# An RWKV-7 and sliding-window block on one core: the recurrence's first corner moves behind KB's products, and the moments ahead of its copy

## The reference, cut to what matters

```python
def step(S, inp):
    r_t, w_t, k_t, v_t, kk_t, a_t = inp
    sa = jnp.einsum('bhvk,bhk->bhv', S, -kk_t)
    S = (S * w_t[:, :, None, :]
         + sa[..., None] * (kk_t * a_t)[:, :, None, :]
         + v_t[..., None] * k_t[:, :, None, :])
    return S, jnp.einsum('bhvk,bhk->bhv', S, r_t)
...
mean = jnp.mean(o, axis=-1, keepdims=True)
var = jnp.mean(jnp.square(o - mean), axis=-1, keepdims=True)
o = ((o - mean) * lax.rsqrt(var + GN_EPS)).reshape(B, T, W)
```

## Time and profile before

| | us |
|---|---|
| runs, lowest, median, highest of 3 | 1305.36, 1310.01, 1314.89 |
| profiled execution | 1319.53 |
| its span in the trace | 1317.7 |
| TensorE busy (share of the span) | 1269.1 (96%) |
| VectorE busy | 829.4 (63%) |
| ScalarE busy | 480.1 (36%) |
| GpSimd busy | 271.8 (21%) |
| mean granted clock of TensorE | 0.975 of full speed |

### The profile page before, as it was taken

One profiled execution on the slowest core, in us unless ns is written; L12 is line 12 of the kernel. 1 busy time (PEld: TensorE's weight loads), 2 busy tenths in 40 slices (PEclk: granted clock), 3 DMA queues, 4 the chain that ended last, 5 costly groups with the idle time before them and its releaser, 6 DMA issues.

```text
span 1317.7 us, 20551 instructions
## 1 busy us (share of the span) xinstructions
PE 1269.1 (96%) x8207; PEld 1040.8 (79%) x8207; DVE 829.4 (63%) x1247; ACT 480.1 (36%) x863; POOL 271.8 (21%) x210
## 2 busy tenths in 40 slices
PE   7999999989899999999999999999999999999996
PEld 6888888655688888778878888888888887888885
DVE  6856522289766877364485665666777676546765
ACT  6100033398422323233463333333333334333334
POOL 0465600034311112110003332233133200000001
PEclk9999999999987989699999999999999999999998
DMA  5576532300222232152213223214544577766643
GB/s 217 186 250 219 209 116 93 109 1 18 48 57 48 52 72 58 31 204 106 80 49 128 70 74 96 96 55 154 176 154 150 192 241 270 257 206 215 208 144 136
DMA packets 117627, 172.80 MB, mean 131 GB/s; under 512 B 55328, under 2 KB 59424, under 8 KB 117280
## 3 DMA queue, kind: packets, MB, share of 16 engines
q1 hardware_dynamic: 117536, 171.54, 39.4%
HBM read 119.57 MB, written 51.39 MB: 130 GB/s over the span
## 4 chain that ended last, share of the span: by engine, by line
PE 80%; DVE 9%; DMA 5%; ACT 3%; issue 2%; POOL 0%; SPq 0%; DVEq 0%; ACTq 0%; POOLq 0%
PE bank L2366 28%; PE bank L363 21%; PE bank L2470 14%; PE bank L468 2%; PE bank L1491 2%; PE bank L1416 2%; DMA hid_scratch<-rt 1%; PE bank L377 1%; PE bank L1262 1%; DMA inv_scratch<-LM 1%; DMA X<-inv_scratch 1%; PE bank L986 1%; DVE scores L1172 1%; PE bank L1497 1%; DMA v_scratch<-vo 1%
## 5 line engine op out<-in xcount | busy, mean ns | idle before, releaser
L2366 PE MATMUL bank<-thi,ahi 128*128 128x512 f32 x320 | 124.5, 389 | 0.0
L2366 PE MATMUL bank<-tlo,ahi 128*128 128x512 f32 x320 | 124.5, 389 | 0.0
L2366 PE MATMUL bank<-thi,alo 128*128 128x512 f32 x320 | 124.5, 389 | 0.0
L2470 PE MATMUL bank<-ch,dwh 128*128 128x512 f32 x308 | 120.4, 391 | 1.3 <-DVE dwl L2044 1.2
L2470 PE MATMUL bank<-ch,dwl 128*128 128x512 f32 x308 | 119.9, 389 | 0.0
L2470 PE MATMUL bank<-cl,dwh 128*128 128x512 f32 x308 | 119.9, 389 | 0.0
L342 DVE TENSOR_TENSOR ring_wlo<-ring_raw,ring_whi 128x1024 fp32r<-128x1024 f32 x30 | 40.1, 1336 | 124.4 <-ACT ring_whi L336 124.4
L363 PE MATMUL bank<-hhi,ring_whi 128*128 128x512 f32 x288 | 114.8, 399 | 0.0
L363 PE MATMUL bank<-hhi,ring_wlo 128*128 128x512 f32 x288 | 112.4, 390 | 0.0
L363 PE MATMUL bank<-hlo,ring_whi 128*128 128x512 f32 x288 | 112.3, 390 | 0.0
L2366 PE MATMUL bank<-x1hi,ahi 128*128 128x512 f32 x240 | 93.4, 389 | 0.0
(11 more groups left out here) (341 smaller groups left out, 2826.7 us busy)
## 6 DMA issues: line engine op xcount, KB each, us to landing
hraw<-hid_scratch SPq DMA_DIRECT2D x12, 1024.0 KB, 6.5
hid_scratch<-hid SPq DMA_DIRECT2D x22, 512.0 KB, 6.2
hid_scratch<-rt SPq DMA_DIRECT2D x11, 1024.0 KB, 4.9
dwr<-down_sums SPq DMA_DIRECT2D x16, 704.0 KB, 4.3
ring_raw<-in_w_in SPq DMA_DIRECT2D x20, 512.0 KB, 4.1
raw_a<-in_w_gate_up SPq DMA_DIRECT2D x20, 512.0 KB, 4.1
raw_b<-in_w_gate_up SPq DMA_DIRECT2D x20, 512.0 KB, 4.8
dwr<-in_w_down SPq DMA_DIRECT2D x12, 704.0 KB, 4.5
```

Source lines behind the costliest of these rows:

```text
L2366: mm = pe.matmul(b[:, :], w[:, k, :], m[:, k, :], start=opens and k == 0 and i == 0, stop=not (j, n) in parts and k == 3 and i == 2, skip_ ...
L2470: mm = pe.matmul(b[:, :], w[m % 2][:, k, :], a[:, k, :], start=opens and k == 0 and i == 0, stop=name not in PART2 and k == KF - 1 and i = ...
```

## The change

Three things move and one goes. On TensorE, for tiles from 1 on, KB's products into R and the claim of O's bank come ahead of the first corners, and half of O's products comes right behind them, ahead of the first updates; until now it came behind the cumulative sums. This is the order that tile 0 had already. On VectorE, the moments of tile `t - 1` come ahead of the copy of the first corners, and its variance ahead of the read of the first updates. In the last tile two fillers stand behind the state product where three stood.

```diff
                 if not more:
                     C.emptied(pe, "S", t - 1)
-                    busy(bank[3], 3)
-                if t:
-                    corners(1, t)
+                    busy(bank[3], 2)
                 pe.wait_ge(s_vtk, 16 * t + 16)
                 for g in range(4):
                     C.emptied(pe, f"k{g}", t)
                 products_of(br, 1, *range(H)).then_inc(s_r, 1)
                 bo = C.claim(pe, "O", t)
+                corners(1, t)
+                products_of(bo, 0, *range(4))
                 if t == 0:
-                    corners(1, t)
-                    products_of(bo, 0, *range(4))
                     busy(C.claim(pe, "S", t), 1)
                 pe.wait_ge(s_xt, 32 * t + 32)
                 updates(1, t)
                 if t + 2 < NT:
                     cumulative(pe, t + 2)
-                if t:
-                    products_of(bo, 0, *range(4))
                 corners(2, t)
...
             for t in range(NT):
+                if t:
+                    moments(t - 1)
                 first_corners(t)
                 if t:
-                    moments(t - 1)
+                    variance(t - 1)
                 first_updates(t)
-                if t:
-                    variance(t - 1)
                 if t + 2 < NT:
```

## The result

The changed kernel takes 1344.64 us (median of 4 runs, 1340.93 to 1347.42) against 1311.13 us before: a ratio of 1.027, interval 1.022 to 1.032. It is slower by 33 us. The forecast was 1315, within 1297 to 1327. Its profiled execution took 1344.65 us, span 1342.9, mean granted clock 0.951.

What follows compares the result with a forecast made beforehand. A ring through VectorE and a DMA bounds clean tiles, TensorE itself slowed ones. From the 1310 us median, -2 for the order of work and +7.4 for one more clock fall gave 1315, range 1297 to 1327.

Steps and rivals of the forecast that it cites:

- KB's products, the claim, the half of O's products: TensorE, ahead of the first updates: corner waits for VectorE's moments, updates 1.72 us behind its start, 0.45 us later than before.
- The sum for the order of work: All changes of order in the eight-tile recurrence at equal clock: -1.9, rounded -2 us, from +3 to -6.
- A clean tile, -0.4: Tile at full clock: updates +0.45 us, masks 0.8 sooner after them, -0.35, say -0.4; clean tiles of 23.8 us.
- The wait ahead of the second KB masks: VectorE's 0.85 us wait for TensorE in a clean tile would close, ending the masks 0.8 us sooner after the updates.
- Variance, filler, last tile, -1.5: Last tile: one filler less, earlier variance and GpSimd, second corner and updates sooner; together -1.5 us (0 to -2.5).
- one fall more, +7.4 us: TensorE's clock in the recurrence: one more drop to half speed than the three before, +7.4 us; chance 0.36.
- the tiles behind a slowed one: Tiles 2 and 5 had no wait ahead of the corner and kept their clock; the new order adds 0.7 us.
- The price of a fall: Cost over a clean tile of a tile with TensorE's clock at half: 7.4 us each, 22 for three.
- many falls: Rival: the claim's pause slows two or three more of six tiles, +16.5 us, 1323 to 1330; chance 0.19.
- one directly behind another: Profile sign of the rival with two or three extra falls: clock at half in five or more tiles, consecutively.
- The rule on idle time: Skill ties mid-kernel clock drops to TensorE idling; shorter waits could then only reduce falls, 1301 instead of 1315.

Runs made afterwards that it cites:

- experiment 3: Changed kernel with one filler between KB's products and the claim of O's bank, ahead of the corner, in tiles 1 to 7; 1315.7 us.
- experiment 6: Changed kernel with one filler a tile behind half of O's products, between corner and updates, the wait ahead of the corner left; 1314.5 us.
- experiment 1: Kernel before with VectorE's half of the change alone (moments ahead of the corner's copy, variance ahead of the first updates' read); 1310.0 us.
- experiment 10: Changed kernel with three fillers behind the state product of the last tile, as before, instead of two; 1339.6 us.
- 7: Changed kernel with the moments of each tile on VectorE behind the masks of KB instead of those of b; 1307.3 us.
- 2: Changed kernel with the claim of O's bank and half of O's products back behind the cumulative sums from tile 1 on; 1336.2 us.

## Why the prediction was wrong

It had the direction and named what the clock would do, but put the number of added falls at one where it was four.

- **KB's products, the claim, the half of O's products.** Right in kind. The wait is ended by `oc`, it is 0.73 us (forecast 0.7 behind a slowed tile), the updates stand 1.74 us behind the corner (1.72). The sum for the order of work was -2 us; the base gives -1.5, but anything from 0 to -3 fits, so this is in agreement and not a proof.
- **A clean tile, -0.4.** There was none in the changed kernel. With the clock kept up it was 0.5 us shorter with the filler in it (experiment 3), and an estimated 23.5 us without it (experiment 6), against 24.15: -0.5 to -0.7. In experiment 6 the masks come 0.9 us sooner after the updates (forecast 0.8). The stretch from the masks' end (434.14) to the updates is 2.95 us without the filler, against 2.83, so 0.1 us longer and not 0.45. The wait ahead of the second KB masks that was to close stayed at 0.75 us.
- **Variance, filler, last tile, -1.5.** VectorE's half (experiment 1) and the filler (experiment 10) have little weight; no run measures the -1.5 by itself.
- **The clock: this step failed.** I wrote "I take one fall more, +7.4 us". The reasons ahead of it were borne out: the tiles behind a slowed one lost what set them apart, and fewer products stand between corner and updates. I then set against them that a clean tile stands still for 0.6 us instead of 1.28, and cut the added falls from 1.5 to one. The stretch has to be taken as a whole. Before, the 1.28 us of standing were followed by a corner and sixteen products ahead of the updates; in the changed order the products end first, and pause, corner, eight products and updates follow. All seven tiles fell, four more than in the profile of before. The price of a fall was right: the four added 65 us at half clock in this stretch, 16 each, which at 0.42 is 6.8 us against 7.4. Four falls at 7.4 less 2 would have given 1338. The rest is where I counted from: the profiled execution of before had 66 us at half clock, the median of its runs 52, and those 14 us are worth 6. In the medians it is 133 us against 52, 34 us. The rival "many falls" named the sign, "one directly behind another", but stopped at 2.5 extra falls and 1330. Its chance of 0.19 was small for what came, and the range ended at 1327, 18 us short of the 1345 measured.
- **The rule on idle time.** The Trainium skill, TensorE: Matmul & The Clock Gate, Why this matters for your kernels, ties such drops to TensorE standing idle. Ahead of the corners TensorE stood still for 4.4 us in the changed kernel's profile, in six pauses of 0.73 or 0.74 us, and for 5.0 in that of before, in four of 1.13 to 1.37. The falls were more all the same. In experiment 6 the six pauses were as long as in the changed kernel and 52 us at half clock were left. The measurement decides: idle time alone doesn't tell.

Left open is why the filler in the last two tiles takes 35 us at half clock off experiment 3 (58 to 17 and 23) and nothing off 7 and before (48 to 44, 52 to 47). In their profiles a fall in one tile seems to shift where the next ones come, so that falls are not independent, but no run here shows that by itself. Open, too, is how far the bases of kernels with few runs (changed, 2 and 10, four each) would move with more.

## What to carry to other kernels

Where the clock of TensorE falls in a latency-bound loop, split every run into time at half clock and the base before reading any difference; here the base moved by 1.5 us and the clock by 34. When work is moved ahead of a wait, look at what is left behind the wait: here a pause, and then small products and only eight larger ones up to the updates, cost 34 us, while the six pauses come to 4.4. A filler in such a pause, or moving what ends the pause, is cheap to try; they took 29 and 37 us off the changed kernel. Against the kernel before, those two versions gained nothing; one filler in the kernel before gained 0.5%, and fillers in two places of the changed one 0.7%. And a profiled execution is one draw: the one of before was 9.5 us slower than the median, so count falls in more than one run before pricing them.

## What the runs showed of the hardware that I had not expected

The time follows the time at half clock almost alone: 0.44 us per us over 94 runs of one kernel. It would be 0.50 if TensorE were the limit throughout and each of its instructions took twice as long at half clock (an estimate from the two levels). Of the first updates at least the second doesn't hold: their first row took 1.08 us for 0.72.

In the changed kernel the clock fell in each of six tiles with a pause of 0.73 us ahead of the corner, while TensorE was busy for 94 to 98% of each of them. With a filler behind the corner and the same pause it held in three of six and fell for only 3.4 us in two more. A busy share close to one is no sign that the clock will hold.
